# Two of four k-blocks of the conv branch's output product in three float32r products, inside the attention stage of a decoder step

## What is computed

```python
def conv_branch(u_hist, conv_w, conv_b, ln_g, ln_b, w_conv_out):
    y = lax.conv_general_dilated(u_hist, conv_w[:, None, :], ...) + conv_b
    y = jax.nn.silu(layer_norm(y, ln_g, ln_b))
    return jnp.einsum('bsc,cd->bsd', y, w_conv_out)      # 512 channels -> 1024, float32
...
s = jnp.einsum('bqkgd,bqnkd->bqkgn', qg, k_sel) * (HEAD_DIM ** -0.5)
p = jax.nn.softmax(jnp.where(valid, s, -inf));  o = jnp.einsum('bqkgn,bqnkd->bqkgd', p, v_sel)
```

## Time and profile before

| | us |
|---|---|
| median of three runs (2721.18 to 2724.5) | 2724.31 |
| the profiled execution's own time | 2722.72 |
| its span, first to last instruction | 2721.0 |

### The profile page before, as it was taken

How to read it: one execution, slowest core, us unless ns; L and a number is a source line. 1 busy time by engine, 2 the same in 40 slices (tenths; PEclk the granted TensorE clock), 3 DMA queues, 4 the chain that set the end, 5 groups by cost and what they waited for, 6 DMA issues and landing times. The chain is left out here.

```text
span 2721.0 us, 46479 instructions
## 1 busy us (share of the span) xinstructions
PE 2588.0 (95%) x16292; PEld 1692.4 (62%) x16293; DVE 1989.8 (73%) x3029; ACT 1553.2 (57%) x2634; POOL 855.9 (31%) x1053
## 2 busy tenths in 40 slices
PE   8999999999999989999999988999999699999988
PEld 6766888987999945655456655455555444444433
...
GB/s 125 109 54 62 139 111 124 60 83 40 130 138 135 141 108 78 84 22 20 76 50 28 37 121 297 256 144 151 228 169 77 154 375 337 346 321 328 326 248 286
DMA packets 241758, 416.11 MB, mean 153 GB/s; under 512 B 31284, under 2 KB 156988, under 8 KB 232586
## 3 DMA queue, kind: packets, MB, share of 16 engines
...
## 5 line engine op out<-in xcount | busy, mean ns | idle before, releaser
L557 PE MATMUL p_ps_acc<-p_x_hi,p_w_hi 128*128 128x352 f32 (+2 forms) x1480 | 526.9, 356 | 1.8 <-DVE p_x_lo L861 1.7
L557 PE MATMUL p_ps_acc<-p_x_lo,p_w_hi 128*128 128x352 f32 (+2 forms) x1480 | 518.0, 350 | 0.0
L557 PE MATMUL p_ps_acc<-p_x_hi,p_w_lo 128*128 128x352 f32 (+2 forms) x1480 | 517.8, 350 | 0.0
L902 DVE SCALAR_TENSOR_TENSOR g_shared<-g_late,p_taps,g_shared 128x1024 f32<-128x1024 f32 x360 | 435.1, 1236 | 8.5
L557 PEld LDWEIGHTS p_ps_acc<-p_x_hi,p_w_hi 128*128 128x128 f32 (+1 forms) x1480 | 275.9, 186 | 50.3 <-issue 21.3
L557 PEld LDWEIGHTS p_ps_acc<-p_x_lo,p_w_hi 128*128 128x128 f32 (+1 forms) x1480 | 276.1, 187 | 26.6 <-issue 0.5
L557 PEld LDWEIGHTS p_ps_acc<-p_x_hi,p_w_lo 128*128 128x128 f32 (+1 forms) x1480 | 275.6, 186 | 27.0
L3596 PE MATMUL e_ps_G<-l_wgu,e_xT 128*32 x656 | 290.7, 596 | 1.0 <-ACT e_xT L3657 1.0
L3596 PE MATMUL e_ps_G<-g_shared,e_xT 128*32 128x512 f32 x656 | 290.3, 595 | 0.0
L3596 PE MATMUL e_ps_G<-g_late,e_xT 128*32 128x512 f32 x1312 | 290.2, 595 | 0.0
L480 POOL CAST p_w_hi<-g_late 128x1024 fp32r<-128x1024 f32 x74 | 97.2, 1314 | 597.3 <-PE p_ps_acc L557 578.4
...
## 6 DMA issues: line engine op xcount, KB each, us to landing
...
l_wgu<-in_w_gate_dram SPq DMA_DIRECT2D x32, 1024.0 KB, 12.0
l_wgu<-in_w_up_dram SPq DMA_DIRECT2D x32, 1024.0 KB, 14.8
l_wd<-in_w_down_dram SPq DMA_DIRECT2D x30, 1024.0 KB, 12.4
...
g_late<-featT SPq DMA_DIRECT2D x54, 256.0 KB, 5.6
```

The source lines that it names most:

```text
L557: m = nc.tensor.matmul(bank(n, tb)[0:rows, 0:width], wp[:, slot, k, 0:rows], xp[:, k, at], start=(k == 0 and i == 0), stop=(k == KD - 1 an ...
L902: ch.mark(nc.vector.scalar_tensor_tensor(dst, src, wt, dst, ALU.mult, ALU.add))
```

## The change

Of the four channel blocks of a unit, two (channels 256 to 511) stay float32 products; the other two (channels 0 to 255) become three float32r products each. For this:

- `y_hi`, `y_lo` (tokens) are made by VectorE once for each token block, in `split_tokens`, at the end of slots 0, 9, 22 and 37 (ROUND_AFTER): one copy and one subtraction of 128x1024.
- `wc_hi` is made by ScalarE (`round_weights`, a copy of 128x256), `wc_lo` by VectorE (`split_weights`, a subtraction of 128x256), once for each unit. ScalarE rounds unit i+1's weights at the end of `keep_branch(i)`; VectorE takes the remainder in the next slot, behind `largest`.
- A unit's weights come in two loads of 128 KB. The part that is rounded is loaded one slot behind unit i-2 for unit i (`load_next`, between the two `exp`), the other part in `keep_branch` as before. Both lie in free columns of `c.late`.
- `conv_b`, `oT_st`, `o_raw` and `o_sb` have one buffer instead of two, with waits on the use before. The store of a unit is issued at the start of the next slot.
- The units move: slot 0 and slot 37 lose theirs, slots 20 and 46 get one, and in slot 38 the unit goes from the middle to the end.

```diff
-BRANCH_SLOTS = [0, 1, 2, 3, 4, 5, 6, 7, 8, 10, 11, 12, 14, 15, 18, 19, 23, 27, 31, 32, 33, 34, 35, 36, 37, 38, 39, 40, 41, 43, 44, 45]
+BRANCH_SLOTS = [1, 2, 3, 4, 5, 6, 7, 8, 10, 11, 12, 14, 15, 18, 19, 20, 23, 27, 31, 32, 33, 34, 35, 36, 38, 39, 40, 41, 43, 44, 45, 46]
+ROUND_AFTER = {0: 0, 9: 1, 22: 2, 37: 3}
...
                 def branch(i):
                     n = at.turns["c", i]
                     bank_free(n)
-                    pe.wait_ge(y_loaded, 16 * (i // 8 + 1))
-                    pe.wait_ge(wc_loaded, 16 * (i + 1))
-                    for k in range(CB):
-                        m = nc.tensor.matmul(ps_t[n % 3][:], wc_blk[:, k, :], y_blk[:, k, :], start=(k == 0), stop=(k == CB - 1))
+                    pe.wait_ge(y_loaded, 16 * (i // KD + 1))
+                    pe.wait_ge(wc_whole, 16 * (i + 1))
+                    for k in range(2):
+                        nc.tensor.matmul(ps_t[n % 3][:], wc_blk[1][:, k, :], y_blk[:, 2 + k, :], start=(k == 0), stop=False)
+                    pe.wait_ge(y_split, i // KD + 1)
+                    pe.wait_ge(wc_split, i + 1)
+                    for k in range(2):
+                        nc.tensor.matmul(ps_t[n % 3][:], wc_hi[:, k, :], y_hi[:, k, :], start=False, stop=False)
+                        nc.tensor.matmul(ps_t[n % 3][:], wc_lo[:, k, :], y_hi[:, k, :], start=False, stop=False)
+                        m = nc.tensor.matmul(ps_t[n % 3][:], wc_hi[:, k, :], y_lo[:, k, :], start=False, stop=(k == 1))
                     m.then_inc(t_full, 1)
...
+                def load_next(i):
+                    if i < 4 * KD:
+                        act.wait_ge(wc_split, i)
+                        load_weights(i, 0, wc_loaded)
+
...
+                def round_weights(i):
+                    act.wait_ge(wc_loaded, 16 * (i + 1))
+                    nc.scalar.copy(wc_hi[:], wc_blk[0]).then_inc(wc_rounded, 1)
...
                 def keep_branch(i):
                     n = at.turns["c", i]
-                    if i >= 2:
-                        act.wait_ge(conv_stored[i % 2], 16 * (i // 2))
+                    if i:
+                        act.wait_ge(conv_stored[(i - 1) % 2], 16 * ((i - 1) // 2 + 1))
                     act.wait_ge(t_full, n + 1)
-                    nc.scalar.copy(conv_b[:, i % 2], ps_t[n % 3][:]).then_inc(t_kept, 1)
+                    nc.scalar.copy(conv_b[:], ps_t[n % 3][:]).then_inc(t_kept, 1)
                     load_branch(i + 1)
-                    store_branch(i - 1)
+                    if i + 1 < 4 * KD:
+                        round_weights(i + 1)
 
                 act.wait_ge(c.y_stored, 16 * len(PARTS))
                 load_branch(0)
+                load_weights(0, 0, wc_loaded)
+                round_weights(0)
                 exp(0, 0)
                 exp(0, 1)
                 for g in range(NSLOT):
                     if g % 4 == 0 and g:
                         keep_raw(g // 4 - 1)
                     keep_turned(g, 0)
+                    if g - 1 in BRANCH_AT:
+                        store_branch(BRANCH_AT[g - 1])
...
                     if g + 1 < NSLOT:
                         exp(g + 1, 0)
+                    if g == 0:
+                        load_next(1)
+                    if g - 1 in BRANCH_AT:
+                        load_next(BRANCH_AT[g - 1] + 2)
...
+                def split_tokens(q):
+
+                    raw = y_blk[:, 0:2, :]
+                    dve.wait_ge(y_loaded, 16 * q + 16)
+                    nc.vector.tensor_copy(y_hi[:], raw).then_inc(y_rounded, 1)
+                    dve.wait_ge(y_rounded, q + 1)
+                    nc.vector.tensor_tensor(y_lo[:], raw, y_hi[:].bitcast(F32), ALU.subtract).then_inc(y_split, 1)
+
+                def split_weights(i):
+
+                    dve.wait_ge(wc_rounded, i + 1)
+                    if i:
+                        dve.wait_ge(t_full, at.turns["c", i - 1] + 1)
+                    nc.vector.tensor_tensor(wc_lo[:], wc_blk[0], wc_hi[:].bitcast(F32), ALU.subtract).then_inc(wc_split, 1)
+
                 dve.wait_ge(made, 1 + HALVINGS + 1)
                 masked(0, 0)
                 largest(0)
+                split_weights(0)
...
                     if g + 1 < NSLOT:
                         largest(g + 1)
+                    if BRANCH_AT.get(g - 1, 4 * KD) + 1 < 4 * KD:
+                        split_weights(BRANCH_AT[g - 1] + 1)
```

More of the change, by code:

```diff
@@ L1400, in attend_prompt @@
     with Phase(nc, "q_") as ph:
[L1401 removed]
+        oT_st = ph.sb("oT_st", [P, 4, P])
         q_st, qi_st = query_tiles(c)
@@ L1412, in attend_prompt @@
         y_blk = c.late[:, 4 * D:6 * D].rearrange("p (k t) -> p k t", k=CB)
-        wc_blk = ph.sb("wc_blk", [P, CB, P])
-        conv_b = ph.sb("conv_b", [P, 2, 512])
+        wc_blk = [c.late[:, (i + 1) * T - 2 * P:(i + 1) * T].rearrange("p (k f) -> p k f", k=2) for i in range(2)]
+        y_hi, y_lo = (ph.sb(n, [P, 2, 512], F32R) for n in ("y_hi", "y_lo"))
+        wc_hi, wc_lo = (ph.sb(n, [P, 2, P], F32R) for n in ("wc_hi", "wc_lo"))
+        conv_b = ph.sb("conv_b", [P, 512])
         sm = ph.sb("sm", [P, 2, 2, T])
         pT = ph.sb("pT", [P, 2, NT, P])
-        o_raw = ph.sb("o_raw", [P, 2, 4, P])
-        o_sb = ph.sb("o_sb", [P, 2, 4, P])
+        o_raw = ph.sb("o_raw", [P, 4, P])
+        o_sb = ph.sb("o_sb", [P, 4, P])
         pow2 = ph.sb("pow2", [P, HALVINGS])
@@ L1658, in count_y, with load_weights @@
                                              accum_out=count[:, j % 4, r:r + 1]).then_inc(counted[1], 1)
-                def load_branch(i):
-                    if i < 32:
-                        if i % 8 == 0:
-                            act.dma_start(y_blk[:], c.yT[:, (i // 8) * 512:(i // 8) * 512 + 512].rearrange("(k p) t -> p k t", p=P)).then_inc(y_loaded, 16)
-                        act.dma_start(wc_blk[:], c.inp["w_conv_out"][0][:, (i % 8) * P:(i % 8 + 1) * P].rearrange("(k p) f -> p k f", p=P)).then_inc(wc_loaded, 16)
+                def load_weights(i, part, landed):
+                    rows = c.inp["w_conv_out"][0][part * 2 * P:(part + 1) * 2 * P, i % KD * P:(i % KD + 1) * P]
+                    act.dma_start(wc_blk[part], rows.rearrange("(k p) f -> p k f", p=P)).then_inc(landed, 16)
@@ L1860, in _ @@
                     behind(g, 5)
+                    if g in ROUND_AFTER:
+                        split_tokens(ROUND_AFTER[g])
                 normalise(NT - 1)
```

49 lines of the change are left out of this document (26 added, 23 removed).

## The result

| | before | after |
|---|---|---|
| median of five runs, us | 2724.5 | 2743.2 |
| lowest and highest | 2721.18 to 2730.28 | 2736.98 to 2747.17 |
| the profiled execution's span | 2721.0 | 2745.5 |

The ratio is 1.0064, 95% interval 1.0049 to 1.0080: the change made the kernel 0.64% slower, 17 us (13 to 22). The two profiled executions lie further apart than that, by 24.5 us: the one after is the slowest of its five.

A forecast was written before the change was run, and what follows sets the result against it. VectorE or ScalarE was taken to bound the earlier windows, TensorE plainly only the last; start +6.5 and windows +1, +1.5, -0.6, +3, -0.5 sum to +10.9 on 2724.3, so 2735 us, range 2714 to 2745.

The forecast's parts named there:

- third rival: ScalarE's wait for weights costs about 0.8 us in each of 20 neighbouring slots, on top of the forecast: 2745 us; 14%.
- recorded signs: Trace signs named beforehand for right or wrong: first `exp` time, VectorE's waits for TensorE, the rounding copy's wait, unit length.
- The start: Before slot 0: rounding the first unit's weights waits for their load and delays `exp(0, 0)`; +6.5 us (+2.5 to +8).
- The products: Units on TensorE: 3.21 us instead of 3.63, saving 0.42 each, 13.4 us of TensorE's time over 32 units.
- The first window: Slots 0 to 11: VectorE's added 8.6 us replace its waits, so TensorE's saving buys nothing; +1 us (-2 to +4).
- The second window: Slots 12 to 22: ScalarE gets 7.5 us, VectorE 4.5 and TensorE 1.1 more; +1.5 us (0 to +3.5).
- ScalarE's wait for the weights: Slots 32 to 35 among others: the rounding copy waits 1.3 us for a load issued between the two `exp`.
- fourth window: Slots 32 to 37: ScalarE's net 8.4 us of additions against 5.3 us idle; +3 us (0 to +6).
- The third window: Slots 23 to 31: saving of three units against three pieces on VectorE; -0.6 us (-1.3 to +0.5).
- The last window: Slots 38 to 46, bound by TensorE: its -1.1, with ScalarE's additions fitting idle time; -0.5 us (-1.5 to +3).
- Single buffers: One buffer instead of two for four buffers: waits on earlier uses cost nothing, at most 1 us once.
- The first rival: TensorE bounds throughout, so its 18.7 us come back whole: 2712 us, faster; 14%.

The follow-up runs named there:

- e1: The kernel before, with ScalarE waiting for the first unit's weights ahead of exp(0, 0); ratio 1.0033 (1.0021 to 1.0045), +9 us.
- e4: The changed kernel with each unit's last two blocks as one float32 product each instead of six float32r ones; ratio 1.0097 (1.0076 to 1.0118), +26 us on the kernel before.
- e5: The kernel before, float32 and two buffers kept, with only the changed kernel's unit places; ratio 1.0018 (1.0005 to 1.0030), +5 us.
- e3: The changed kernel with nothing ahead of exp(0, 0) and the weights' remainder right behind `masked`; ratio 1.0036 (1.0024 to 1.0048) to the kernel before, +10 us.
- e8: The kernel before with one unit moved from slot 39 to slot 42, all products float32; ratio 1.0011 (0.9996 to 1.0027).

## Why the prediction was right, and where its terms were not

The forecast was 2735 with a range of 2714 to 2745, slower at 64%; 2743.2 was measured. Sign and range held; the forecast's own narrower range, 2729 to 2741, did not. The sum was +10.9 and the measurement +17 (13 to 22), so I read the terms. They say that part of the hit is luck. The largest term was right in kind, but in the trace the first and the last window lost 4 us more than forecast each and the fourth 4 us less, and the third rival, whose mechanism never occurred, had the nearer figure, 2745. Of the recorded signs, the late first `exp` and the unit of 3.2 us came true, and so did, but for 5.1 us in slot 8, the end of VectorE's waits for TensorE in the first window (5.5 us, twice). One of the signs of being wrong came true as well: the rounding copy never waits for its load after the start.

- **The start, +6.5: right, a little small.** 8.0 in the trace; e1's wait alone gives 6.1 at slot 0 and 5.7 at slot 9. The mechanism was read from the right rows. What I left at the edge of the range, the table load behind the wait, happened. This is the largest term of the loss.
- **The products, 0.42 us each: right in size.** A unit now takes 1366.79 - 1363.49 = 3.30 us in slot 36 against 3.63. What the saving is worth is shown by e4: nothing in slots 0 to 8, as forecast, and about 0.3 us for a unit from slot 13 on.
- **The first window, +1: mis-sized, +5.4** (13.4 less 8.0 at slot 12's mark) **and the wrong place.** VectorE's added pieces cost almost nothing in slots 0 to 8 (0.6 us in all), against 90% busy: the 1.2 us "left over" were right. What failed was the step that dealt with what the change makes wait. I had asked who waits behind ScalarE's rounding, and not who waits for VectorE's remainder. `split_weights` stands behind `largest`, and in slot 8 VectorE has the sums and the range search ahead of that, visible in the trace of before. TensorE waited 8.9 us in eight places, 3.25 in slot 8, 2.10 in slot 11 and 1.81 in slot 39.
- **The second window, +1.5: +3.5.** 2.4 of it are the end of the same step, in slot 12; then 1.5 are won by slot 21, and slot 20's unit costs 2.2 (2.6 in e5).
- **ScalarE's wait for the weights, 1.3 us in slots 32 to 35, fourth window +3: wrong, -1.4.** The rounding waited for its load once, at the start. In slot 32:

```profile
1327.80 0.37 ACTq L1672 DMA_DIRECT2D g_late<-in_w_conv_out_dram  x1
1328.04 1.59 ACT L1667 ACTIVATE q_junk_act<-g_early,q_mid 128x1536 bf16<-128x1536 f32 x1
1329.60 0.63 ACT L1660 ACTIVATE q_sm<-q_sm,q_negmax 128x384 f32<-128x384 f32 x1
1331.41 0.41 ACT L1688 CAST q_wc_hi<-g_late 128x256 fp32r<-128x256 f32 x1
```

  `load_next` stands behind the first `exp` in the program, and the issue left 1.8 us before that `exp` began, ahead of the count before it too. In slot 33 it was 2.1 us (1336.77 against 1338.86). I had let the issue start with the `exp`. With 3.6 us to the rounding no wait is left, and the size of the fixed part of a transfer didn't matter. The third rival, built on that wait, falls with it.
- **The third window, -0.6: +0.3.** Right within its bounds.
- **The last window, -0.5: +3.8, and 3.2 more by slot 48.** Mis-sized, and the failed step is in the moves. I had booked "put slot 38's unit last" as a gain, the wait for its load, and had not asked what it does for TensorE where it stood. e5 prices it, in a kernel without any splitting: 3.5 us, since the unit had run in a gap that TensorE has anyway, and 4.8 for all moves together. `split_tokens` behind slot 37 stands right ahead of `masked(39, 0)` and goes with 2.1 us of the step. The 3.2 us by slot 48 are slot 46's unit, which the forecast had at its full length.
- **Single buffers, nothing:** no wait of the stage names a store, and TensorE's for `o_raw` are 0.3 us.
- **The first rival**, TensorE's 18.7 us whole, is refuted by e4: of the products' 13.4 us, 3.8 show.

If the parts simply add, which no run shows, the trace has 8.0 for the start, 4.8 for the moves (e5), 22.7 in all, so 9.9 for the splitting itself after what the products save; e3 takes 6.6 of it away by slot 13 by nothing but an earlier remainder, and 4.1 by the end. After the stage the two executions come 1.5 us nearer again, for which I have no cause, and single profiles of the same code differ by up to 5.6 us where `front` ends. The runs say 17 us, not the 21 that these two traces differ by behind `front`, so the steps are somewhat too large as a whole; the clock that the kernel before kept in slot 8 can be up to 1.8 of that.

What stays open: why the clock falls in one execution and not in another with the same wait, and so how much of the steps at slots 9 and 38 another execution of the kernel after would show. None of the versions was faster than the kernel before; e8 alone can't be told from it (0.9996 to 1.0027).
